# First block's attention alone, with z's products ahead of it: one change to a three-block kernel on Trainium2

## What is computed

```
q, kc, vc, ks, vs, kw, vw, z, gl = split(h @ w_in_b)
for each head: three attentions with ALiBi slopes and one query
    cmp: over 31 compressed keys      slc: over the selected keys      win: over a causal window
o = g0 * o_cmp + g1 * o_slc + g2 * o_win        # g = sigmoid(gl)
y = o * silu(z)                                  # z = h @ w_z, 512 x 1024
merged = sigmoid(h @ w_gate) * (y @ w_branch)
```

## Time and profile before

| | us |
|---|---|
| median of 3 runs (lowest, highest) | 3525.58 (3520.84, 3527.49) |
| the profiled execution's own time | 3527.07 |
| its span from the first to the last instruction | 3525.3 |
| TensorE busy over the span | 3099.6 (88%) |
| ScalarE, VectorE, GpSimd busy | 1155.9, 1102.4, 1278.1 |
| mean granted TensorE clock | 0.913 |
| the phase of the change, first scores to the next phase's first product | 230.92 to 494.15 |

### The profile page before, as it was taken

The page is one execution under the profiler, slowest core; times in us unless marked ns, Lnnn a source line. Parts: engine busy times, 40 slices in busy tenths (PEclk is TensorE's granted clock), DMA queues, the critical chain, the costliest instruction groups (busy, mean ns, idle before and its releaser), DMA issues. The chain is left out here.

```text
span 3525.3 us, 45177 instructions
## 1 busy us (share of the span) xinstructions
PE 3099.6 (88%) x17513; PEld 2536.8 (72%) x17513; DVE 1102.4 (31%) x2526; ACT 1155.9 (33%) x2127; POOL 1278.1 (36%) x622
## 2 busy tenths in 40 slices
PE   5889989989699789999999899998976569889998
PEld 3765558878678576676879899996834538768877
DVE  4126650221211204663534222101026931222210
ACT  3237662222142223433534222222234133323321
POOL 3232224444255231221225354443401326735543
PEclk8889999999899897999989899999977569999999
DMA  6220013323233120112224123232200014423332
GB/s 225 94 63 19 13 32 94 97 85 93 72 90 93 51 66 29 36 49 90 74 76 158 61 83 95 84 96 70 86 19 9 1 30 133 131 66 95 95 90 95
DMA packets 78874, 267.85 MB, mean 76 GB/s; under 512 B 9597, under 2 KB 9853, under 8 KB 78576
## 3 DMA queue, kind: packets, MB, share of 16 engines
q1 hardware_dynamic: 76328, 262.52, 24.0%
q10 hardware_dynamic: 2376, 3.00, 0.2%
HBM read 256.88 MB, written 8.61 MB: 75 GB/s over the span
## 5 line engine op out<-in xcount | busy, mean ns | idle before, releaser
L157 POOL TENSOR_TENSOR weights_lo<-weights_raw,weights_hi 128x1024 fp32r<-128x1024 f32 x430 | 1031.6, 2406 | 1259.3 <-ACT weights_hi L149 1258.8
L195 PE MATMUL acc<-h_hi,weights_hi 128*128 128x512 f32 (+1 forms) x2120 | 745.5, 352 | 73.4 <-PEq L87 71.9
L196 PE MATMUL acc<-h_lo,weights_hi 128*128 128x512 f32 (+1 forms) x2120 | 743.3, 351 | 0.0
L197 PE MATMUL acc<-h_hi,weights_lo 128*128 128x512 f32 (+1 forms) x2120 | 743.0, 350 | 0.0
L149 ACT ACTIVATE weights_hi<-weights_raw 128x1024 fp32r<-128x1024 f32 x430 | 453.4, 1057 | 811.5 <-PE acc L197 463.0
L195 PEld LDWEIGHTS acc<-h_hi,weights_hi 128*128 128x128 f32 x2120 | 403.7, 190 | 128.5 <-issue 77.6
L196 PEld LDWEIGHTS acc<-h_lo,weights_hi 128*128 128x128 f32 x2120 | 404.0, 191 | 50.8
L197 PEld LDWEIGHTS acc<-h_hi,weights_lo 128*128 128x128 f32 x2120 | 403.7, 190 | 50.9
L807 PE MATMUL acc<-h_hi,weights_hi 128*128 128x264 f32 (+1 forms) x768 | 272.2, 354 | 18.0 <-PEq L604 10.1
L808 PE MATMUL acc<-h_lo,weights_hi 128*128 128x264 f32 (+1 forms) x768 | 250.1, 326 | 0.0
L809 PE MATMUL acc<-h_hi,weights_lo 128*128 128x264 f32 (+1 forms) x768 | 249.8, 325 | 0.0
(11 more groups left out here) (400 smaller groups left out, 5068.9 us busy)
## 6 DMA issues: line engine op xcount, KB each, us to landing
weights_raw<-in_stream SPq DMA_DIRECT2D x430, 512.0 KB, 3.6
weight_ring<-in_w_ada SPq DMA_DIRECT2D x24, 512.0 KB, 12.6
gates<-gate_tiles SPq DMA_DIRECT2D x24, 264.0 KB, 4.5
gate<-gates SPq DMA_DIRECT2D x8, 792.0 KB, 5.6
flipped<-bias_rows SPq DMA_DIRECT2D x8, 320.0 KB, 5.0
x<-in_x ACTq DMA_DIRECT2D x1, 2048.0 KB
w<-in_w_cmp SPq DMA_DIRECT2D x1, 2048.0 KB, 7.2
out<-x SPq DMA_DIRECT2D x1, 2048.0 KB, 7.1
```

The costliest lines, as they stand in the source:

```text
L157: pool.tensor_tensor(self.lo[:, at % CUT, :], self.raw[:, at % RAW, :], self.hi[:, at % CUT, :].bitcast(F32), ALU.subtract).then_inc(self. ...
L195: pe.matmul(accs[half], w_hi, x_hi[:, cols], start=start, stop=False)
L196: pe.matmul(accs[half], w_hi, x_lo[:, cols], start=False, stop=False)
L197: last = pe.matmul(accs[half], w_lo, x_hi[:, cols], start=False, stop=stop)
```

## The change

z's eight chunks are made by a `project` stage ahead of the tables and the attention, and the attention phase runs without the lane of products. The chunks' place in the weight stream stays the same (between those of `project_tokens` and those of `gated_output`). The new order writes the distances' slot first, then all slots of the attention.

```diff
         project_tokens(nc, ws, 3, h, S, take)
+        project(nc, ws, KT, [(h, KT, P)], 1, S, copies(z, 1, S), unroll=4)
         distance = sbuf("distance", [P, TAB])
...
-            def keep(i):
-                return lambda act, piece, acc: act.activation(z[:, i, :], acc, ACT.Copy)
-
-            dense = Dense(sem, psum, ws, [unit for i in range(KT) for unit in feature_units(ws, i, h, 1, S, act=keep(i))], KT)
             attention = PairAttend(sem, sbuf_of, psum, k, groups, False, S, tables=(build_tables, [per * n for n in range(NH // 2)]), score_sets=2)
-            run_lanes(nc, [2] + paced((dense.weights, 0, 1), (attention.weights, 0, 1)), [dense, attention, Distances()])
+            run_lanes(nc, [1] + [0] * attention.slots, [attention, Distances()])
```

## The result

The changed kernel takes 3533.13 us (median of 11 runs, 3530.53 to 3540.51), the kernel before 3525.58 (11 runs, 3518.35 to 3527.61). The ratio is 1.0028, with a 95% interval of 1.0018 to 1.0037: slower by 6 to 13 us. The medians lie 7.6 us apart, the ratio's middle is 9.9; both are above the 0.2% that can be told, the interval's lower end just under it.

A forecast was written before the change was run, and what follows sets the result against it. TensorE was taken to bound the first block's attention; +47.0 for the stage, -44.1 for removed steps and +5.4 for returning waits gave +8.3 us, forecast 3534 us, range 3527 to 3546.

The forecast's parts named there:

- TensorE is the bound and a step costs 0.70 us: First block's attention: three products lengthen a slot by 0.70 us; removing 63 such steps gives -44.1 us.
- The stage, +47.0: New eight-chunk projection ahead of the attention: +47.0 us, between 46.6 and 48.0, with about 4 us at half clock.
- The waits that come back, +5.4: Attention: transposes' waits for ScalarE that dense steps hid return, +5.4 us, between 0 and about 9.
- Rival 1: Attention: transposes' waits stay short with ScalarE relieved; +2.9 us, 3528.5, middle pairs of 25.2 us; chance 0.15.
- Rival 2: Attention: ScalarE's chain bounds the phase, so its removed work is a gain; -10.2 us, 3515.4; chance 0.06.
- The opening wait, 0: Attention's start, pairs waiting for the first distance tables: 9.18 us taken as unchanged, at most 3.6 us longer.
- The first pair, -4.5: Attention's first head pair: shorter by 4.5 us without its dense steps, 1.1 us of returning waits included, clock rise unchanged.
- rival 3: Attention: clock rises late or falls; first pair wholly at half clock +16 us, 3550; whole attention some 3690; chance 0.15.
- the rival of a phase at half clock throughout: Whole first-block attention falls to half clock: eight pairs at +20 us, some 3690; within the late-clock rival's chance of 0.15.
- VectorE as a new chain: Attention: VectorE's weights may be late for transposes; up to +0.5 us a pair, +4, counted within the forecast's range.

## Why the prediction was right, point by point

The forecast was 3534 us and +8.3; the medians gave 3533.13 and +7.6. The mechanism is the one that was forecast, and its terms for the stage, the middle pairs and the tail came within a microsecond. That the total came this close is in part luck: the first pair missed by 2.8 us, the opening wait and the middle pairs made up 1.8 of that, and the profiled executions also differ by several microseconds outside the phase.

*TensorE is the bound and a step costs 0.70 us.* Shown: 190.20 us for six pairs with 48 steps that hide nothing, against 156.6 for six without.

*The stage, +47.0.* It took 47.07 at a mean clock of 0.96, which is about 4 us at half as assumed. A stage of the same shape elsewhere in the kernel was the right row.

*The waits that come back, +5.4.* In the middle pairs a dense-free pair took 26.1 us, where the pair that hides nothing, less its steps, gave 26.25; the six saved 30.57 and not 29.7. Rival 1, by which the waits would stay hidden once ScalarE is relieved, had 25.2 and falls: they are set by ScalarE's copy of the transpose before, and the two kernels with moved steps, 6.6 and 18.3 us of such waits, show that place alone brings them back or takes them away. Rival 2, a phase bound by ScalarE, falls with it.

*The opening wait, 0.* It became 0.9 us shorter, and 0.8 in the second pair of executions (9.05 and 8.27). The tables' loads were issued 1.56 us behind a weight load before and 2.69 behind one now; that this is the cause is only argued.

*The first pair, -4.5.* This term was off: -1.72 between the two profiles, because the half-clock stretch was 16.95 us and not 8.55. The prediction took an unchanged rise of the clock and priced a late one in rival 3, as some 2 us for 4 us more at half; for 8.4 us more that is 4.2. Rival 3's sign, a clock under 0.85 in the first pair, came out, at 0.73. But how much of it is the change's is not settled: one more execution of each kernel, the changed one first, had 31.76 us and 35.86, which would be -4.1.

```profile
280.55:312.31 31.76, 28.85 (x180) 15.72 (x180) 21.56 (x112) 21.70 (x84) 9.45 (x8) 0.74 0.01 2
...
235.50:271.36 35.86, 33.67 (x204) 19.13 (x204) 21.65 (x112) 22.83 (x85) 11.84 (x9) 0.79 0.05 16
```

The step that failed is to have read a stretch that varies by 6 us between executions from one execution, and to have left out that behind the new stage the clock falls only inside the opening wait. What the phase added was +9.7 in the first pair of profiles and +6.9 in the second (272.33 and 265.40), 8.3 on average; that two executions average to the sum is no proof of it.

*The clock during the attention.* The granted clock was 1.00 over the six dense-free pairs in three executions, so the rival of a phase at half clock throughout falls. The Trainium skill ("TensorE: Matmul & The Clock Gate", Part 4: PE-mode transpose) says that transposes do not count for the clock as products do; the prediction drew from it that the clock might fall there, and it stayed at 1.00 in all 156.62 us. That does not refute the rule itself, since scores and weighings kept TensorE busy beside the transposes. What set the slow rise no run here shows.

*VectorE as a new chain.* Not in the changed kernel: of 22.2 us that its transposes waited, 19.9 were for ScalarE's copy. Transposes do wait for VectorE elsewhere, as in the pair of 33.10 us, where its scalings were slow beside a GpSimd remainder.

*The signs and the range.* By its letter one sign of being wrong came out: a stretch outside the phase, the second block, changed by 2.9 us, where 2 was the limit. It differs by 6.4 us between the two executions of the kernel before, so the limit was set without knowing the spread. The range's upper end of 3546 does not follow from what it names: the upper ends of the stage and the waits give 3538.5 and a clock 10 us late 3539; only all of them, with 3.6 us for the opening wait, come near it.

## What to carry to other kernels

Products interleaved with a TensorE-bound chain are not free filler: each costs its own time less the wait that it stands in front of, so read where the engine still waits and put the work there, or into the idle opening of a phase. Moving such work to a stage of its own neither saves nor costs much by itself; what it cost here is an opening wait without cover (6.1 us with the stage's end) and the slow clock behind that wait (6.2). And a stretch at half clock behind an idle time should be read from several executions before it enters a sum.

## What the runs showed of the hardware that was not expected

Behind an idle stretch TensorE can be busy without a gap in the profile and still be held at half clock for long: 13.00 of 13 us in the changed kernel, and 13.60 of 13.60 with three dense steps among them.

```profile
289.00:302.00 13.00, 13.00 (x56) 5.77 (x53) 7.20 (x40) 7.16 (x29) 0.69 (x1) 0.50 0.01 3
...
239.10:252.70 13.60, 13.60 (x48) 6.64 (x49) 5.27 (x27) 5.07 (x21) 2.54 (x2) 0.50 0.14 40
```

The products of a projection at the same clock had it back within 3 us. At full clock the same mixture holds it, over all 156.62 us of the six middle pairs. In the kernel with all products first the clock also held through the slow start of the first pair, in which it fell in the kernels with nine and with fourteen steps there:

```profile
278.50:281.90 3.40, 2.23 (x18) 1.43 (x17) 1.98 (x16) 2.26 (x10) 0.00 (x0) 1.00 0.51 154
```
